# Group 0 load order, w_in in column halves, and the output bias on GpSimd

## The reference, cut to what matters

```python
D_MODEL, SEQ, CONV_CH, N_Q_HEADS, HEAD_DIM, D_FF, MEM_LEN = 1024, 4096, 512, 8, 64, 2816, 256
h = rms_norm(x, g_mix)
u = h @ w_in + b_in                    # 1792 columns: conv value|gate | q | k | v
y_conv = silu(layer_norm(depthwise_conv31(a * sigmoid(gate)) + b_dw))
y_attn = windowed_gqa_with_sink(rope(q), rope(k), v, sink)     # |i - j| <= 128
x = x + (concat(y_conv, y_attn) @ w_out + b_out)
x = x + memory_cross_attention(rms_norm(x), rms_norm(mem), w_mem_q, w_mem_kv, w_mem_o)
x = x + (silu(rms_norm(x) @ w_gate) * (rms_norm(x) @ w_up)) @ w_down
out = rms_norm(x, g_final)
```

## Time and profile before

| | us |
|---|---|
| median of 3 runs | 2018.51 |
| lowest and highest | 2016.75, 2023.31 |
| the profiled execution, time | 2009.25 |
| its span on the slowest core (core 2) | 2008.0 |
| its spans on the 8 cores | 1985.2 to 2008.0 |
| PE busy | 1846.9 (92%) |
| DVE / ACT / POOL busy | 1109.5 / 873.2 / 120.6 |

### The profile page before, as it was taken

One profiled execution on the slowest core, in us unless ns is written; L12 is line 12 of the kernel. 1 busy time (PEld: TensorE's weight loads), 2 busy tenths in 40 slices (PEclk: granted clock), 3 DMA queues, 4 the chain that ended last, 5 costly groups with the idle time before them and its releaser, 6 DMA issues.

```text
span 2008.0 us, 34383 instructions; the slowest of 8 cores (1985.2 to 2008.0 us)
## 1 busy us (share of the span) xinstructions
PE 1846.9 (92%) x11516; PEld 974.5 (49%) x11516; DVE 1109.5 (55%) x2430; ACT 873.2 (43%) x1761; POOL 120.6 (6%) x206
## 2 busy tenths in 40 slices
PE   4989998863389999999999999999999999999997
PEld 2545557741135444544454455445444544544443
DVE  5657666553257546643854485467447644754442
ACT  4535534531155444544545354544445453545210
POOL 2100100000100000000000000000001000000000
PEclk7999998766699999999999999999999999999999
DMA  8898865789763316322622363163326223431542
GB/s 263 209 198 217 176 165 168 148 180 194 124 94 127 124 38 235 114 92 79 231 96 93 124 208 116 46 217 119 103 79 219 97 90 132 168 103 56 188 142 100
DMA packets 80934, 284.71 MB, mean 142 GB/s; under 512 B 7159, under 2 KB 38777, under 8 KB 62872
## 3 DMA queue, kind: packets, MB, share of 16 engines
q1 hardware_dynamic: 73592, 237.74, 37.0%
q0 software_dynamic: 2560, 27.99, 10.6%
q10 hardware_dynamic: 4608, 16.78, 2.0%
HBM read 273.16 MB, written 65.10 MB: 168 GB/s over the span
## 4 chain that ended last, share of the span: by engine, by line
PE 78%; DMA 7%; DVE 5%; issue 5%; SPq 3%; ACT 2%; DVEq 0%; ACTq 0%; POOL 0%; POOLq 0%
PE bank L369 52%; PE bank L1447 15%; PE bank L377 5%; DMA arena<-s_y 3%; SPq L359 3%; PE bank L778 2%; PE bank L1086 2%; DMA s_v<-arena 1%; DMA arena<-w_in 1%; PE bank L512 1%; ACT arena L390 1%; PE bank L1090 1%; DVE arena L1368 1%; DVE arena L1056 1%; DVE arena L1211 0%
## 5 line engine op out<-in xcount | busy, mean ns | idle before, releaser
L369 PE MATMUL bank<-arena 128*128 128x512 bf16 (+1 forms) x5724 | 1274.7, 375 | 13.3 <-DVE stat L394 6.6
L369 PEld LDWEIGHTS bank<-arena 128*128 128x128 bf16 x5724 | 555.1, 98 | 616.0 <-issue 38.8
L1447 PE MATMUL bank<-arena 128*128 128x512 bf16 x1408 | 323.2, 379 | 0.6 <-DVE arena L1458 0.6
L390 ACT ACTIVATE arena<-arena 128x1024 bf16<-128x1024 f32 x130 | 137.2, 1055 | 298.5 <-DVE arena L1458 148.6
L377 PE MATMUL bank<-ident,arena 128*128 128x128 bf16 x2080 | 158.1, 224 | 85.3 <-DVE arena L1211 27.2
L1120 ACT ACTIVATE arena<-bank,asm 128x384 bf16<-128x384 f32 (+1 forms) x256 | 146.8, 573 | 145.1 <-DVE asm L1108 128.8
L1447 PEld LDWEIGHTS bank<-arena 128*128 128x128 bf16 x1408 | 133.7, 98 | 149.6 <-issue 7.5
L1413 ACT ACTIVATE arena<-bank 128x512 f32<-128x512 f32 x176 | 105.3, 598 | 229.5 <-PE bank L369 229.0
L377 PEld LDWEIGHTS bank<-ident,arena 128*128 128x128 bf16 x2080 | 137.3, 100 | 130.4 <-issue 98.3
L1104 DVE TENSOR_REDUCE asm<-bank 128x1 f32<-128x384 f32 (+1 forms) x256 | 139.2, 544 | 64.1 <-PE bank L1090 55.0
L1211 DVE TENSOR_TENSOR arena<-bank,arena 128x512 f32<-128x512 f32 x128 | 88.3, 690 | 153.7 <-PE bank L369 122.1
(11 more groups left out here) (85 smaller groups left out, 1292.9 us busy)
## 6 DMA issues: line engine op xcount, KB each, us to landing
arena<-s_gu SPq DMA_DIRECT2D x88, 1024.0 KB, 4.9
arena<-x SPq DMA_DIRECT2D x64, 512.0 KB, 9.2
arena<-s_wd SPq DMA_DIRECT2D x32, 1024.0 KB, 5.0
out<-arena ACTq DMA_DIRECT2D x32, 512.0 KB, 4.0
arena<-s_wd SPq DMA_DIRECT2D x16, 768.0 KB, 4.2
s_gu<-w_gate_up POOLq DMA_DIRECT2D x11, 1024.0 KB, 13.5
s_mem<-w_memory POOLq DMA_DIRECT2D x8, 1024.0 KB, 13.4
arena<-s_mem SPq DMA_DIRECT2D x8, 1024.0 KB, 8.3
```

The costliest lines, as they stand in the source:

```text
L369: ins = nc.tensor.matmul(out_ap, l, r, start=(k == 0), stop=(k == n - 1))
L390: sc.op("act", lambda: nc.scalar.activation(junk, src, AF.Square, accum_out=st[:, 0:1]), reads=[srcb], writes=[junkb, stb], cost=1.26)
L1447: sc.op("pe", lambda t=t, bk=bk: nc.tensor.matmul(bk[:], actT[c][:, t * P:(t + 1) * P], w3[:, c - c0, :], start=(c == 0), stop=(c == NFC - ...
```

## The change

- `w_in` is staged and cast in two column ranges, 0 to 767 (q, k, v) and 768 to 1791 (conv). All first ranges are loaded ahead of x tile 1, all second ranges behind it. A projection waits only for the range it reads, and the q, k, v projections of tiles 0 and 1 are both put ahead of the conv projections of tile 0.
- `bout_pad` holds the bias in all 128 rows (one broadcast DMA, no memset). The bias matmuls are gone from `proj`. In their place `badd`, one GpSimd `tensor_tensor` of 128x1024 per tile, adds the bias to the x tile in place, `after` the tile's `pv` matmuls.
- The x tiles of even groups now lie at 56 to 72 KB, those of odd groups at 105 to 121.
- `gate` is the last matmul of group 0's first output projection (t=0). The first four `ring_load`s and group 1's loads (q, k, v, y and x) wait for it. Before, the ring loads waited for the loads of `WO` and of the last y tile of group 0. Group 1's y loads also get a slack of 40.
- `pace`, which hangs a cast on the last operation made, is called behind the projection instead of ahead of it.

```diff
-    for k in range(4):
-        load_win(k)
+    for k in range(KC):
+        load_win(k, 0)
     load_x(1)
-    for k in range(4, KC):
-        load_win(k)
+    for k in range(KC):
+        load_win(k, 1)
...
-    sc.op("dve", lambda: nc.vector.memset(bout_pad[:], 0.0), writes=[cb2])
-    dma("pool", bout_pad[0:1, :], b_out_d.unsqueeze(0), [], [cb2], bosem)
+    dma("pool", bout_pad[:], b_out_d.partition_broadcast(P), [], [bo_b], bosem)
...
-        o = sc.op("pe", mm_group(bk[:, 0:w], pairs), reads=[cb2, bpad_b, hb] + [w_[1] for w_ in w_in], writes=[bkb], cost=pe_cost(9, w))
+        o = sc.op("pe", mm_group(bk[:, 0:w], pairs), reads=[cb2, bpad_b, hb] + w_in_b[0 if c0 < 768 else 1], writes=[bkb], cost=pe_cost(9, w))
...
-        bq, bqb = a_proj(n, 0, 512)
-        bkv, bkvb = a_proj(n, 512, 256)
-        a_rope(n, bq, bqb, bkv, bkvb)
-        if n > 0:
-            a_qk(n - 1)
+        for n_ in {0: (0, 1), 1: ()}.get(n, (n,)):
+            bq, bqb = a_proj(n_, 0, 512)
+            bkv, bkvb = a_proj(n_, 512, 256)
+            a_rope(n_, bq, bqb, bkv, bkvb)
+            if n_ > 0:
+                a_qk(n_ - 1)
...
-    xres = [[mk((105, 56)[s_] + 4 * t, 4, F32, D) for t in range(4)] for s_ in range(2)]
+    xres = [[mk((56, 105)[s_] + 4 * t, 4, F32, D) for t in range(4)] for s_ in range(2)]
...
-            dma("sp", qT.rearrange("p a n -> p (a n)"), s_q[g], [q_g[g]], [qT_b], qT_sem, (), 0.0 if g else 30.0)
+            dma("sp", qT.rearrange("p a n -> p (a n)"), s_q[g], [q_g[g]], [qT_b], qT_sem, gate if g == 1 else (), 0.0 if g else 30.0)
...
-        yl_last[0] = dma("sp", ybuf(g, t)[0], ..., yt_sem[t % 2 + (2 if g == 0 and t > 1 else 0)])
+        yl_last[0] = dma("sp", ybuf(g, t)[0], ..., yt_sem[t % 2 + (2 if g == 0 and t > 1 else 0)], gate if g == 1 else (), 40.0 if g == 1 else 0.0)
...
+            def badd():
+                sc.op("pool", lambda: nc.gpsimd.tensor_tensor(xs[t][0], xs[t][0], bout_pad[:], ALU.add), reads=[bo_b], writes=[xs[t][1]],
+                      cost=2.2, after=[st["pvo"]])
+                note("x", g, t)
+            add(t0 + 13.2, badd, seen("xl", g, t))
...
-                if bias:
-                    pairs = [(ones_pad[:], bout_pad[:, u * 512:(u + 1) * 512])] + pairs
...
             def a():
+                st["b"] = proj(t, WO, [WO_b], lambda k: ymixT[:, k, t * P:(t + 1) * P], ymc_b + [yma_b[t]])
+                if g == 0 and t == 0:
+                    gate.append(sc.ops[-1])
                 pace(g)
-                st["b"] = proj(t, WO, [WO_b], lambda k: ymixT[:, k, t * P:(t + 1) * P], ymc_b + [yma_b[t]], True)
...
     for j in range(NSLOT):
-        ring_load(j, [wo_op, yl_last[0]])
+        ring_load(j, gate)
```

56 lines of the change are left out of this document (31 added, 25 removed).

## The result

The changed kernel took 2028.3 us (median of 13 executions, 2022.3 to 2129.1) beside 2020.9 us for the kernel before on the same chip (13 executions). The ratio is 1.0038, 95% interval 1.0021 to 1.0054: 0.4% slower, where 1953 us was forecast. The profiled execution took 2028.0 us; its cores' spans go from 1993.6 us (core 2) to 2026.8 us (core 5).

The account below looks back on a forecast made before the run. PE was taken to bound the 185 us FFN periods, and waits with full DMA engines the stretch from 443 to 587 us. Terms 27 + 11 + 9 + 5 + 13 = 65 us off 2018.5 gave 1953 us, range 1935 to 1986.

Parts of the forecast that it names:

- x at 56 KB: Group 0's residual on VectorE: the wait for a late x tile goes, 27 us gained (bounds 20 and 27).
- Fewer loads ahead of y: SP's queue before group 0's first statistics: 1.57 MB less ahead of y, 11 us gained (bounds 0 and 15.49).
- Group 1's y no longer in front: VectorE's order in group 0: slack 40 puts group 1's y statistics later, 9 us gained (bounds 5 and 12).
- The gate: Ring and group 1 loads behind group 0's first output projection: nothing moves, no cost; DMA backlog until 567 covered by the ring.
- The second case: Rival, start of the FFN: DMA engines become the bound and ring slots run dry; 1979 us, with more 1990; chance 0.14.
- The third case: Rival, group 0: x still late or VectorE's order puts another far transfer there, 27 us stay; 1980 us; chance 0.09.
- The halves: w_in at the start: q, k, v projections of tiles 0 and 1 fill PE's hole, 5 us gained (bounds 0 and 7).
- Bias matmuls: PE in the full periods: 56 matmuls of 0.22 us go, group 0's 8 add 1; 13 us gained (bounds 8 and 14).
- The add: GpSimd's bias pass per tile, 2.5 us, between pv matmuls and residual: 5 us of cover, so nothing on the path.
- The slower rival: Full periods: GpSimd's add holds up VectorE's line 1140 scalings or FFN evictions, 98 us; 2051 us; chance 0.05.

Follow-up runs that it names:

- e3: Kernel before with only the x places exchanged (group 0's x at 56 KB): 2018.4 us, ratio 1.0000.
- e13: Kernel before with only the gate, the slack of 40 for y and the later pace of the casts: 2021.4 us, ratio 1.0025.
- e1: Kernel before with only w_in's loads, conversions and projections in column halves: 2033.5 us, ratio 1.0051.
- e16: Kernel before with w_in loaded in whole rows, but converted in column halves and projected in the halves' order: 2020.4 us, ratio 1.0003.
- e8: Changed kernel with w_in in whole rows again, without column halves: 2021.9 us, ratio 1.0044 to the kernel before.
- e19: e2 with GpSimd's pass started behind the first transpose of the probabilities instead of behind their product with the values: 2003.1 us, ratio 0.9939.
- e18: e14 with GpSimd's pass started behind the first transpose of the probabilities: 1981.0 us, ratio 0.9819.
- e2: Kernel before with only the output bias moved to GpSimd, without bias matmuls: 1993.2 us, ratio 0.9898.
- e14: Kernel before with bias on GpSimd, group 0's x at 56 KB, group 1's statistics after group 0's last hTf eviction, four casts earlier: 1984.3 us, ratio 0.9847.
- e17: e2 with GpSimd's pass over each x tile three times as long: 2081.0 us, ratio 1.0326.

## Why the prediction was wrong, step by step

**x at 56 KB, 27 us.** The reading of the wait was right, and it went. The failed step is "Next late behind them is what ran from 521.42 on", which took the wait as removed, not as moved. Alone it is worth nothing (e3): 33.6 us of waiting for group 1's y tile appear. The trace of before already held the sign. The late x tile landed at 521.3 us there, and group 1's first two y tiles at 522.0 and 522.6, from the same queue; right behind the residual that had waited, VectorE ran their statistics:

```profile
522.82 1.28 DVE L1018 BATCH_NORM_STATS2 bnst<-arena 128x6 f32<-128x512 f32 x2
```

With x there in time, the same VectorE order waits for y instead. And the place was not the only reason for the lateness: e13 has the old places and no x wait. Waits in one stretch with full DMA engines are one sum and not three.

**Fewer loads ahead of y, 11 us.** Right on core 2 by the wait: 15.49 us became 3.73, 11.8 us; the statistics themselves came 19.7 us earlier there, more than was forecast. Over the cores the first statistics came 5 us earlier only, after a convolution that ended 5 us later; in e13, without the halves, they came 14 us earlier.

**Group 1's y no longer in front, 9 us.** This is the step that failed most. A slack of 40 in the planner was read as 40 us of real distance. The load of the tile can't go before the gate (465 us on core 2) and landed at 557, 92 us later, so the planner still put its statistics in front of group 0's last scalings. Instead of -9 us the wait grew by 37 us on core 2, and e13 shows that the gate, with its slack and the later casts, does it without the other parts.

**The gate, nothing.** "Nothing moves" looked at the ring loads, which indeed went out at 465.42 beside 467.93 before. What moved were group 1's x, all four tiles of which had been issued by 425 before, and y, which had been issued at about 477 and left at 505. The backlog was computed as 112 us, until 567, and the last cast landed at 568.9. That is luck in part: all else had landed by 557.8, and that cast was issued only at 558.7, since it hung on an operation behind the long wait. The failed step is what stood in it. The sum asked only whether the ring would run dry, and took 134 GB/s for SP's queue beside casts, from a stretch in which casts ran only part of the time; while they ran it got 53. The second case had the engines right but put its price on the FFN's slots (1979 us).

**The third case** was the mechanism: "VectorE's order puts another far transfer where line 1211 waits", with 0.09 and 27 us. It was a line further on, 49 to 58 us of waiting, and with the other losses gave 2028. With a planner that doesn't know real DMA times it deserved the largest chance of the rivals.

**The halves, 5 us.** "The bytes stay, so the last half arrives at the same time" failed: same bytes, 16 smaller transfers, the last conversion 5.4 us later (e1, e16). The 12 us won at the first projection were gone by the ninth block in both e1 and the changed kernel. Alone the halves cost 0.5%; in the changed kernel this is hidden (e8). Why the convolution ends 5 to 8 us late, rather than level, was not isolated.

**Bias matmuls, 13 us.** The term itself was right (12.2 and 12.6 us in e19 and e18). The changed kernel got 6.6 of it.

**The add, nothing.** Its length was right (2.5 taken, 2.12 us measured). The failed step is "So nothing on the path": it looked at who waits for the pass, and nobody did in the changed kernel (VectorE's residual names PE), but operations that don't wait for it were held by it, for 8.2 us per core, and cost some 6, the amount that came back in e19 and e18. The slower rival had the mechanism and named the wrong lines: the scalings of line 1140 met no pass in the traces of the changed kernel, e2, e14, e17, e18 and e19, and the FFN's evictions, which have one operand in PSUM, did (72 times over the eight cores) and kept their 0.68 us. The rule cited with it, from the Trainium skill, "SBUF — State Buffer", section "Who interferes with whom", named the right kind of operation, one with two SBUF inputs, which line 1115 is; the traces agree.

**Sum.** 27 + 11 + 9 + 5 + 13 = 65 us gained were forecast. At the FFN's start 53 of these were due and 17 us were lost instead; in the periods 12 were due and 6.6 came. The chances of being faster add up to 0.94, where 0.93 was written. What stays open: why e2's FFN starts 12 us earlier than before's and e19's only 4, with one and the same edit but for the place of the pass. The planner's order differs, and a change of some 8 us by the order alone has to be reckoned with for every variant here.

## What to carry to other kernels

Where the DMA engines are full, list every transfer that anyone waits for in the stretch, with the time at which it would land in the queue's order; removing the wait on one only hands it to the next, and a load that is put off until "later" must be checked for who stands behind its reader on an in-order engine. A planner's slack is no distance in real time. When work goes to GpSimd, look for VectorE operations with two SBUF operands that may meet it, not only for those that wait for it, and put the pass where none is due.

## What the runs showed that was not expected

- A load of the hardware queue beside casts of the software queue landed just ahead of one of them, on core 2 of the changed kernel 11 to 20 us after the load before it and almost without regard to its size; 2.9 MB in seven loads landed in 9.7 us as soon as no cast was left.
- SP itself is held while it issues: four x loads took 25.24 us to issue, two y loads 19.89 us, so what is behind them in program order hasn't even been asked for.
- VectorE's pass of two SBUF operands over 128 x 2 elements takes 0.156 us, and up to 1.75 us in the changed kernel when it meets GpSimd's 2.12 us pass. In the kernel with the tripled pass two of VectorE's f32-to-bf16 normalisations of 128 x 512 in SBUF per core took 2.26 us instead of 0.54. In e18, where the pass comes earlier, 16 of SiLU's passes (line 1058 of before, 128 x 512, both operands in SBUF, 0.685 us) met it over the eight cores and took 1.74 us on average; in e19 there were 8, at 2.55 us. Passes with a PSUM operand kept their length (in the changed kernel the copy of the attention result 0.687 us apart from and 0.688 us beside a pass), and so did `bn_stats` (0.684 and 0.685 us).
- GpSimd's pass of 128 x 1024 f32 with two operands took 2124 ns. The Trainium skill, "GPSIMD Engine Reference", section 3.1, has 4497 ns for 2048 columns, by which the estimate was 2.25 us: the measured one is 6% less.
